# Middle levels of a triangular inverse as two 64x64 diagonal blocks, multiplied in pairs of 64x64 array tiles

## The reference

```python
lmat = jnp.where(strict, jnp.einsum('nbhid,nbhjd->nbhij', kb, kc) * decay, 0.0)
sol = lax.linalg.triangular_solve(eye + lmat, rhs, left_side=True, lower=True, unit_diagonal=True)
wc, uc = sol[..., :dk], sol[..., dk:]
...
def step(S, xs):
    v_new = u_i - jnp.einsum('bhck,bhkv->bhcv', w_i, S)
    o = (jnp.einsum('bhck,bhkv->bhcv', q_i * jnp.exp(g_i)[..., None], S)
         + jnp.einsum('bhij,bhjv->bhiv', qk_i, v_new))
    S = S * jnp.exp(g_last)[..., None, None] + jnp.einsum('bhck,bhcv->bhkv', k_dec, v_new)
```

## Time and profile before

| | |
|---|---|
| median of 3 runs | 3663.78 us (3661.72 to 3664.67) |
| span of the profiled execution | 3666.3 us |
| PE busy | 3436.8 us, 94% of the span |
| DVE busy | 2145.4 us, 59% |
| ACT busy | 824.0 us, 22% |
| levels of head 0 | from 147.8 to 246.3 us |
| levels of head 2 | from 527.0 to 642.8 us |

### The profile page before, as it was taken

The page is one execution under the profiler, slowest core; times in us unless marked ns, Lnnn a source line. Parts: engine busy times, 40 slices in busy tenths (PEclk is TensorE's granted clock), DMA queues, the critical chain, the costliest instruction groups (busy, mean ns, idle before and its releaser), DMA issues.

```text
span 3666.3 us, 55811 instructions
## 1 busy us (share of the span) xinstructions
PE 3436.8 (94%) x23099; PEld 3327.9 (91%) x23099; DVE 2145.4 (59%) x4443; ACT 824.0 (22%) x1769; POOL 858.3 (23%) x772
## 2 busy tenths in 40 slices
PE   6999999999999999998999999995599899999998
PEld 5989899999999998987999999994499799999997
DVE  5666768586767676776876777635512433423334
ACT  3333233323242332333010111002200300000001
POOL 2202020202020111201333333322323133333331
PEclk8999999999999999999999999996699899999999
DMA  2111111111111111110112222226611011111111
GB/s 90 56 47 43 58 44 50 55 44 50 41 59 48 54 51 51 47 41 30 49 61 84 72 84 78 71 65 217 180 41 47 29 47 47 47 47 46 47 48 62
DMA packets 111275, 222.60 MB, mean 61 GB/s; under 512 B 24880, under 2 KB 59184, under 8 KB 110000
## 3 DMA queue, kind: packets, MB, share of 16 engines
q1 hardware_dynamic: 82400, 177.66, 15.6%
q10 hardware_dynamic: 28624, 41.38, 3.5%
HBM read 177.86 MB, written 41.14 MB: 60 GB/s over the span
## 4 chain that ended last, share of the span: by engine, by line
PE 86%; DVE 9%; DMA 1%; ACT 1%; issue 1%; SPq 1%; POOL 0%; POOLq 0%; DVEq 0%; ACTq 0%
PE ps L218 31%; PE ps L610 15%; PE ps L1329 14%; PE ps L687 4%; PE ps L782 4%; PE ps L786 3%; PE ps L773 3%; DVE dwork L1254 1%; PE ps L234 1%; PE ps L622 1%; PE ps L662 1%; PE ps L295 1%; PE ps L628 1%; PE ps L637 1%; PE ps L712 1%
## 5 line engine op out<-in xcount | busy, mean ns | idle before, releaser
L218 PE MATMUL ps<-hhi,whi 128*128 128x344 f32 x2424 | 778.6, 321 | 19.6 <-DVE hlo L1798 14.7
L218 PE MATMUL ps<-hhi,wlo 128*128 128x344 f32 x2424 | 775.8, 320 | 0.0
L218 PE MATMUL ps<-hlo,whi 128*128 128x344 f32 x2424 | 775.0, 320 | 0.0
L2059 POOL TENSOR_TENSOR wtick<-wtick 128x1 f32<-128x1 f32 x213 | 58.9, 277 | 2608.6 <-PE ps L218 819.9
L2062 POOL TENSOR_TENSOR wlo<-wraw,whi 128x1024 fp32r<-128x1024 f32 x213 | 533.0, 2502 | 17.1
L218 PEld LDWEIGHTS ps<-hhi,whi 128*128 128x128 f32 x2424 | 457.3, 189 | 22.7 <-issue 16.6
L218 PEld LDWEIGHTS ps<-hhi,wlo 128*128 128x128 f32 x2424 | 456.9, 188 | 0.0
L218 PEld LDWEIGHTS ps<-hlo,whi 128*128 128x128 f32 x2424 | 456.3, 188 | 0.1
L610 PE MATMUL ps<-hhi,whi 128*128 128x344 f32 x1152 | 388.7, 337 | 1.8 <-DVE dwork L1002 1.8
L610 PE MATMUL ps<-hhi,wlo 128*128 128x344 f32 x1152 | 370.8, 322 | 0.0
L610 PE MATMUL ps<-hlo,whi 128*128 128x344 f32 x1152 | 370.3, 321 | 0.0
(11 more groups left out here) (350 smaller groups left out, 6179.7 us busy)
## 6 DMA issues: line engine op xcount, KB each, us to landing
wraw<-in_w SPq DMA_DIRECT2D x213, 512.0 KB, 3.5
dwork<-keep_rows SPq DMA_DIRECT2D x64, 256.0 KB, 3.6
tab<-keep_tab SPq DMA_DIRECT2D x8, 1088.0 KB, 6.2
S<-in_sin ACTq DMA_DIRECT2D x16, 512.0 KB, 3.6
drw<-keep_del SPq DMA_DIRECT2D x32, 256.0 KB, 3.3
out_sout<-S ACTq DMA_DIRECT2D x16, 512.0 KB, 2.7
keep_u<-hs SPq DMA_DIRECT2D x8, 580.0 KB, 3.0
uu<-keep_u SPq DMA_DIRECT2D x8, 580.0 KB, 7.7
```

The costliest lines, as they stand in the source:

```text
L218: ins = nc.tensor.matmul(out, w, r[:, kt, blk(n)], start=k == 0, stop=k == 3 * KT - 1)
```

## The change

Up to the fifth level nothing couples the upper and lower 64 rows of a matrix. After the change, levels 1 to 5 hold the two 64x64 diagonal blocks of each matrix one above the other: `NM`, `PP`, `TT_` and the new `YC` are 128 partitions by 4x64 columns. Each of `P`, `TP`, `PY` and the first transpose is then 8 matmuls of 64x64 by 64 columns (`tiles`), with the upper block in array tile (0, 0) and the lower one in tile (64, 64). Neighbours in the list alternate between the two tiles and write to different banks. A product is drained by one instruction over two banks where there were two, and masks and sums are half as wide. At level 5 the sum is written in two halves into the full-width `Y`, and level 6 uses 64x64 tiles too. A copy of the lower right block beside the upper one is added (`NTc`).

Banks: levels take 0, 1 (P, TP) and 2, 3 (PY, first transpose), the chain moves to 4, and 5 to 7 are left for other slot work. Ahead of a head's first level PE waits for all readers of banks 0 to 3. Two output pieces move to another slot (6 to 8 in quad 0, 6 and 7 to 7 and 8 in quad 2), `Y_1` and `YC` get places of their own, and a small copy of the convolution's taps (`tcw`) goes.

```diff
-        NM, PP, TT_, ATT_0, Y_1, VB, ATT_1, KD, EG, DEC_0, DEC_1, Y_0 = (dwork[:, i] for i in range(12))
+        NM, PP = (dwork[:, 0].rearrange("p a b -> p (a b)")[:, k * 4 * H:(k + 1) * 4 * H].rearrange("p (j n) -> p j n", n=H) for k in range(2))
+        TT_, YC = (dwork[:, 1].rearrange("p a b -> p (a b)")[:, k * 4 * H:(k + 1) * 4 * H].rearrange("p (j n) -> p j n", n=H) for k in range(2))
...
-        DENSE = (0, 1, 2, 4, 5, 6, 7)
-        PIECE_SLOTS = ((0, 1, 2, 3, 4, 6, 7, 9), (0, 2, 3, 4, 6, 7), (0, 3, 4, 6, 7), (0, 3, 4, 6, 7))
+        TILES = [(half ^ h, h, c) for half in range(2) for c in range(2) for h in range(2)]
+        DENSE = (0, 1, 2, 3, 5, 6, 7)
+        LEV_A, LEV_B, CB = (0, 1), (2, 3), 4
+        PIECE_SLOTS = ((0, 1, 2, 3, 4, 7, 8, 9), (0, 2, 3, 4, 6, 7), (0, 3, 4, 7, 8), (0, 3, 4, 6, 7))
...
+            def tiles(banks, col, lhsT, rhs):
+                for half, h, c in TILES:
+                    r = slice(H * half, H * half + H)
+                    ins = nc.tensor.matmul(ps[r, banks[h], col + c * H:col + (c + 1) * H], lhsT(r, 2 * h + c), rhs(r, 2 * h + c), start=True, stop=True)
+                return ins
...
-                    for h in range(2):
-                        p.after(*(("DVE", gq + f"T{l - 1}.{h}") if l > 1 else ("ACT", gq + "T0")))
-                        b = use(h, "ACT", gq + f"P{l}.{h}")
-                        for c in range(QCH):
-                            j = 2 * h + c
-                            ins = nc.tensor.matmul(ps[:, b, c * P:(c + 1) * P], NM[:, j], TT_[:, j], start=True, stop=True)
-                        p.go(ins, gq + f"P{l}.{h}")
+                    p.after(*(("DVE", gq + f"T{l - 1}") if l > 1 else ("ACT", gq + "T0")))
+                    p.go(tiles(LEV_A, COL_P, lambda r, j: NM[r, j], lambda r, j: TT_[r, j]), gq + f"P{l}")
                     slot(i, q, 2 * (l - 1) + 1)
...
+                    p.go(tiles(LEV_A, COL_T, lambda r, j: YC[r, j], lambda r, j: PP[r, j]), gq + f"TP{l}")
+                    p.go(tiles(LEV_B, COL_Y, lambda r, j: PP[r, j], lambda r, j: YC[r, j]), gq + f"PY{l}")
...
+                for b in LEV_A + LEV_B:
+                    p.after(*held[b])
                 for q in range(NQ):
                     levels(i, q)
...
+                v.go(V.tensor_copy(M[H:P, :, 0:H], M[H:P, :, H:P]), g + "NTc")
...
-                                v.go(V.tensor_tensor(TT_[:, hh], pairs(ps[:, h, 256:512]), TT_[:, hh], ALU.add), gq + f"T{l}.{h}")
+                            v.go(V.tensor_tensor(side_by(TT_), both(LEV_A, COL_T), side_by(TT_), ALU.add), gq + f"T{l}")
```

More of the change, by code:

```diff
@@ L638, in gram, with first_t @@
                 p.go(ins, g + "G")
-            def first_t(i, q, bank):
+            def tiles(banks, col, lhsT, rhs):
[3 more added lines that the diff above has]
+                return ins
+            def first_t(i, q):
                 g = f"{i}.{q}."
                 p.after("DVE", g + "Y0")
[L643 to L646, removed]
+                p.go(tiles(LEV_B, COL_T0, lambda r, j: YC[r, j], lambda r, j: idh[r, :]), g + "T0t")
             def chain(i, q, k):
@@ L665, in chain @@
                     p.after("DVE", g + "qg")
-                    b = use(3, "ACT", g + f"o{c}")
+                    b = use(CB, "ACT", g + f"o{c}")
                     for h in range(2):
@@ L672, in chain @@
                     p.after("DVE", g + "kd")
-                    b = use(3, "DVE", g + f"S{c}")
+                    b = use(CB, "DVE", g + f"S{c}")
                     for h in range(2):
@@ L734, in slot @@
                     if q + 1 < NQ:
-                        first_t(i, q + 1, until(0))
+                        first_t(i, q + 1)
                 piece = piece_at(q, s)
@@ L743, in last_level @@
                 Y = YY[q % 2]
-                for h in range(2):
-                    p.after("DVE", gq + f"T5.{h}")
-                    b = use(h, "ACT", gq + f"P6.{h}")
-                    for c in range(QCH):
-                        j = 2 * h + c
-                        ins = nc.tensor.matmul(ps[:, b, c * P:c * P + H], DEC[q % 2][:, j], TT_[:, j, 0:H], start=True, stop=True)
-                    p.go(ins, gq + f"P6.{h}")
+                p.after("DVE", gq + "T5")
+                for j in range(4):
+                    ins = nc.tensor.matmul(ps[H:P, LEV_A[0], j * H:(j + 1) * H], DEC[q % 2][0:H, j, H:P], TT_[0:H, j], start=True, stop=True)
+                p.go(ins, gq + "P6")
                 slot(i, q, 11)
-                p.after("ACT", gq + "P6.1")
+                p.after("ACT", gq + "P6")
                 p.after("DVE", gq + "Y5")
-                b = use(2, "DVE", gq + "Y6")
+                b = aside("DVE", gq + "Y6", (i * NQ + q + 1) * SLOTS)
                 for j in range(4):
-                    ins = nc.tensor.matmul(ps[0:H, b, j * P:j * P + H], PP[:, j, 0:H], Y[:, j, H:P], start=True, stop=True)
+                    ins = nc.tensor.matmul(ps[0:H, b, j * H:(j + 1) * H], PP[H:P, j], Y[H:P, j, H:P], start=True, stop=True)
                 p.go(ins, gq + "PY6")
@@ L760, in levels @@
                 gq = f"{i}.{q}."
-                Y = YY[q % 2]
                 for l in range(1, 7):
@@ L811, in mix_pe @@
                     if k == 3:
-                        first_t(i, 0, take)
+                        for b in LEV_B:
+                            use(b, "ACT", f"{i}.0.T0")
+                        first_t(i, 0)
+                for b in LEV_A + LEV_B:
+                    p.after(*held[b])
                 for q in range(NQ):
                     levels(i, q)
+                held[LEV_A[0]] = ("ACT", f"{i}.{NQ - 1}.P6")
+                held[LEV_A[1]] = ("DVE", f"{i}.{NQ - 1}.T5")
+                for b in LEV_B:
+                    held[b] = ("DVE", f"{i}.{NQ - 1}.Y5")
             e = HQK - 1
@@ L833, in evac @@
                     a.after("DVE", g + f"conv{t - 2}")
-                a.after("DVE", g + "tcw")
                 for n in range(NC3):
@@ L1014, in conv @@
                 v.after("ACT", g + f"cv{t}")
-                w = tcw[:, t]
+                w = cw[:, i, t]
                 o = qkv[:, t, 0:T]
@@ L1279, in mix_dve @@
                     add_x(e, m, n)
-        tcw = m_("tcw", [P, 4, CONVW])
         def rotation(p):
```

127 lines of the change are left out of this document (68 added, 59 removed).

## The result

The changed kernel takes 3634.46 us (median of 4 runs, 3628.22 to 3635.77) against 3664.23 us of the kernel before: ratio 0.9904, interval 0.9889 to 0.9919. It is faster by 30 us where -107 was forecast, and 4 us above the top of the range. The profiled execution has a span of 3634.1 us, 32.2 less than before.

What follows compares the result with a forecast made beforehand. The prediction took the number of passes on PE to bound the levels, with the DVE as next limit. Products -218, visits +116, shorter waits -8 and readers +3 gave -107 off 3663.8, so 3557 us; 8-in-10 range 3500 to 3630.

Steps and rivals of the forecast that it cites:

- The products (-218): PE's level products, P6 and first transposes: 64x64 tiles in pairs at 0.058 us a step save 218 us.
- Rival A: Level products on PE: 64x64 passes run one tile at a time or wait for loads; 3797 us, 13 in 100.
- the rule beside it: Loads on PE: a tile's second load waits for its first pass, a step nearer 0.11 us, result that of Rival A.
- The visits (+116): PE's changes from whole-array work to smaller tiles and back: 335 more at 0.345 us each, +116 us.
- Rival C: PE's layout changes cost little, a third of the price, 34 us in all; about 3475 us, 8 in 100.
- The DVE's share: Narrower sums and masks on the DVE: net some -4.85 us a quad, so it doesn't become the bound.
- Wait for the readers, +3: Ahead of a head's first level PE waits for readers of banks 0 to 3, 0.75 us in four heads: +3 us.
- Shorter waits, -8: Quad 2, laid out by the DVE's order: PE's waits get shorter, 31.5 to about 27.5 us; in all -8 us.
- -139 with 15 to spare: Low end of the forecast's 68-in-100 band: step as taken, visits at 0.25 us, waits a bit shorter; given as 3505.
- Rival B: Levels on PE: saving lost to waits for drains and sums, 0.4 us a level, 64 us; about 3620, 10 in 100.

Runs made afterwards that it cites:

- e5_one_bank: The changed kernel with each product of a level in one PSUM bank instead of two, leaving five banks for other slot work; 3579.5 us.
- e15_gate_later: e5_one_bank with the DVE's two norm products moved behind the chain's sum of slot 6 and their followers one slot later; 3563.4 us.
- e1: The changed kernel with the 64x64 matmuls listed so that the same tile comes four times in a row instead of alternating; 3766.5 us.
- e11: The kernel before with one unread 64x64 matmul of two passes added ahead of every row of the dense stage, 144 in all; 3732.9 us.
- e14: The kernel before with the sample rows' product, passes of 2 columns, done twice in slot 5 of quads 0 and 2; 3722.2 us.
- e10: e5_one_bank with quad 2's output piece in slot 10 and quad 0's piece of slot 8 moved to slot 5; 3596.1 us.
- e13: e5_one_bank with four unread passes of 256 columns added behind the sample rows' product in slot 5 of quads 0 and 2; 3595.5 us.

## Why the prediction was wrong

Lengths of the quads in us, from the last start of one PY6 to that of the next (quad 0 from the end of the dense stage), in heads where the clock held if there were any (quad 2 of the changed kernel has a fall of 1.7 us in every one):

| | quad 0 | 1 | 2 | 3 |
|---|---|---|---|---|
| before | 28.1 | 28.5 | 31.5 | 27.7 |
| changed | 27.9 | 25.1 | 32.3 | 24.6 |
| e5_one_bank | 24.2 | 25.1 | 28.2 | 24.6 |
| e15_gate_later | 24.2 | 25.1 | 27.5 | 23.3 |

**The products (-218): right in their price.** A step of two passes is 0.058, and e1 shows that the order of the list makes it. Without it the change would have made the kernel slower (3766.5 us).

**Rival A and the rule beside it: refuted.** 16 passes take 0.46. The Trainium skill's rule ("TensorE: Matmul & The Clock Gate", "Part 3: Packing small matmuls — row/col tiling") says that a weight load overlaps matmuls in flight only when their row groups differ. In this case's rows loads of one and the same tile follow each other each 0.058 us though each is 0.139 long, within a product as in PY6; the measurement decides. The same section of the Trainium skill says that matmuls in different tiles run concurrently, with starts about 4 ns apart; the pairs of the changed kernel start 6 or 7 ns apart, which agrees.

**The visits (+116): right.** 0.345 was taken, e11 gives 0.33 to 0.35, and the count of 367 is that of the trace. Rival C is refuted.

**The DVE's share: right in size.** Sums, masks and copies of 256 columns take 0.41 to 0.49, and the DVE's busy time fell by 121 us (155 forecast).

**"Wait for the readers, +3": right in size.** Behind the last dense product of a head PE waits for the ACT in six of the heads, 3.4 us in all, against 0.6 before.

**"Shorter waits, -8": wrong. Here the prediction failed.** It laid quad 2 out by the DVE's order alone, as if a piece always had a bank. The diff leaves three banks for slot work where there were four, puts PY6 among them, and moves two pieces; the sum has no term for the first two, and the prediction doesn't speak of the moved pieces. The other term that is missing is one for the granted clock: the prediction read 1.00 in three windows of before and carried it over. What the runs show in the place of both is in the windows over `mix`, of before, the changed kernel and e5 (PE's busy time stands first):

```profile
140.00:1667.60 1527.60, 1468.37 (x10876) 1415.66 (x10874) 1059.71 (x2387) 511.20 (x1134) 228.47 (x174) 0.99 0.15 49
140.00:1630.30 1490.30, 1377.80 (x15096) 1247.05 (x15094) 937.05 (x2280) 442.94 (x941) 226.47 (x174) 0.97 0.16 50
140.00:1573.10 1433.10, 1357.01 (x15098) 1230.78 (x15096) 937.05 (x2282) 442.43 (x942) 226.36 (x174) 0.99 0.17 53
```

PE is idle for 59 us before, 112 in the changed kernel and 76 in e5. So waits rose by 53 us where 5 less were forecast. With each product of the levels in one bank and the same visits, slots and chain (e5), `mix` is 57 us shorter in the profiled executions: 36 us of idle time and 21 us of PE's busy time are gone, 19 of these falls of the clock. The medians differ by 55. So 55 of the 77 us between forecast and result are banks, their waits and the falls that went with them.

**The other 22 us** lie between e5 (-85) and the forecast (-107). In the profiled executions e5 is 94 us ahead of before, 13 short of the forecast, and 12 us of falls (20.5 against 8.5) are nearly all of that. The other nine are there because the profiled execution of e5 is 5 us below its runs' median and that of before 3 to 4 above its own. In both the granted clocks go the same way (e5 0.965 against 0.962, before 0.968 against some 0.971), so the falls account for this too, as far as three digits tell.

That e5 comes so near is in part luck. PE is idle for 17 us more than before, not for 5 less; and its busy time, the 12 us of falls taken off, fell by 123 us where products and visits promised 102. Where these 21 us come from was not followed.

One sum of the prediction is off: -139 with 15 to spare gives a lower bound of 3510, not 3505. Nothing hangs on it.

**Rival B was near**, in that the gain was lost to waits, 3634 measured against its 3620. But its mechanism, drains and sums of the levels that come late, is not what happened: PE waited for the ACT's copy L982 only 7.1 us in the whole program. What grew were the waits of the slot work's pieces, by 31 us for L1092 and L1144.

What stays open: what exactly makes the clock fall in the levels of e5. e14 shows that no wait and no small tile is needed; but neither e10 nor e13, which put wide passes beside those with few columns, had clearly fewer falls. And the dense stages of the changed kernel are together 10 us longer than before, of which the visits for the first transposes explain 2.4 and the falls 1.7; in e5 they are 3.5 longer.

## What to carry to other kernels

When a change gives more PSUM banks to one user, list for every other user which bank it gets at each place and whose read it must then wait for, in the order of the reading engine: here three banks for slot work cost 55 us against five, and each wait named a result (L1092, L1144) that the waiting matmul doesn't use. Count banks before tiles: the same products written to different partitions of one bank needed half the banks at the same speed. And where a change alters what PE runs, read the granted clock over the new kernel, in more than one execution, before trusting busy shares.

## What the runs showed of the hardware

- Two 64x64 tiles run abreast also when both write to one bank on different partitions: a product of 16 passes stays at eight steps of 0.058 us, 0.61 us to the next start with the leaving (e5).
- Going from the whole array to a 64x64 tile and back costs 0.33 us with no wait around it (e11): 0.24 instead of 0.158 us into the first small pass, 0.26 instead of 0.116 for the two small ones, and 0.26 instead of 0.158 into the second pass after.
- The granted clock fell to its lower level, 1.2 GHz, with PE busy for 6.00 of 6 us (0.75 over these 6 us), behind whole-array passes of 2 columns and with no wait (e14, 15 of 16 places). 144 visits in the dense stage didn't bring it down: e11 lost 3.4 us below full clock in `mix`, the kernel before 8.5.
